# Hybrid mixer stack on one Trainium2 core: the mLSTM strand's last head held back until SSD's last masks, in the order of steps that the engines share

## The reference, cut to what matters

```python
x = x + 0.5 * swiglu(rms_norm(x, ffn1_norm[l]), ...)
u = rms_norm(x, mix_norm[l]) @ w_in[l]
y = concatenate([ssd_mixer(u_ssd), mlstm_mixer(u_ml), rwkv7_mixer(u_rw)])
x = x + y @ w_out[l]
x = x + 0.5 * swiglu(rms_norm(x, ffn2_norm[l]), ...)
```

```python
h = num / jnp.maximum(jnp.abs(den), jnp.exp(-m_t))[..., None]
h = h.reshape(bsz, t, H, Dh) * o
return group_rms_norm(h.reshape(bsz, t, MLSTM_WIDTH), norm_g, H)
```

## Time and profile before

| | us |
|---|---|
| time, median of 3 runs | 1778.43 (1778.34 to 1779.82) |
| the profiled execution | 1779.76 |
| its span in the profile | 1777.8 |
| PE busy | 1712.3 (96%) |
| DVE busy | 1292.2 (73%) |
| ACT busy | 931.8 (52%) |
| POOL busy | 409.6 (23%) |

### The profile page before, as it was taken

How to read it: one execution, slowest core, us unless ns; L and a number is a source line. 1 busy time by engine, 2 the same in 40 slices (tenths; PEclk the granted TensorE clock), 3 DMA queues, 4 the chain that set the end, 5 groups by cost and what they waited for, 6 DMA issues and landing times.

```text
span 1777.8 us, 32695 instructions
## 1 busy us (share of the span) xinstructions
PE 1712.3 (96%) x13812; PEld 1538.4 (87%) x13812; DVE 1292.2 (73%) x2137; ACT 931.8 (52%) x1666; POOL 409.6 (23%) x316
## 2 busy tenths in 40 slices
PE   8999999999899999999999999989999999989998
PEld 6888988887798888888898888779888898979987
DVE  5887775856667887688777576566787666789974
ACT  5774435323446764577443532344676445556652
POOL 2772000000213761167200000021376200021110
PEclk9999999999799999999999999989999999989999
DMA  6675622211146664666562221114665543335442
GB/s 253 241 273 192 218 95 96 81 41 49 49 156 254 236 237 173 220 247 224 190 215 95 95 96 32 44 49 168 225 247 200 196 173 119 119 143 187 172 153 105
DMA packets 45057, 282.67 MB, mean 159 GB/s; under 512 B 6128, under 2 KB 6768, under 8 KB 18544
## 3 DMA queue, kind: packets, MB, share of 16 engines
q1 hardware_dynamic: 44912, 280.60, 43.8%
HBM read 279.53 MB, written 1.05 MB: 158 GB/s over the span
## 4 chain that ended last, share of the span: by engine, by line
PE 83%; DVE 11%; ACT 3%; issue 1%; DMA 1%; POOL 0%; SPq 0%; DVEq 0%; ACTq 0%
PE banks L517 27%; PE banks L518 13%; PE banks L1052 8%; PE banks L509 7%; PE banks L511 7%; PE banks L510 7%; PE banks L1659 4%; DVE WL L486 2%; ACT WH L481 2%; PE banks L1928 1%; DVE XC L1121 1%; PE banks L556 1%; DMA ring<-wst 1%; PE banks L1938 0%; PE banks L724 0%
## 5 line engine op out<-in xcount | busy, mean ns | idle before, releaser
L486 DVE TENSOR_TENSOR WL<-ring,WH 128x2048 fp32r<-128x2048 f32 (+1 forms) x223 | 469.0, 2114 | 119.4 <-ACT WH L481 119.2
L517 PE MATMUL banks<-XNP,WH 128*128 128x512 f32 x1408 | 498.6, 399 | 10.8 <-DVE XNP L602 8.6
L481 ACT ACTIVATE WH<-ring 128x2048 fp32r<-128x2048 f32 (+1 forms) x223 | 381.0, 1716 | 59.0 <-PE banks L511 46.6
L518 PE MATMUL banks<-XNP,WL 128*128 128x256 f32 x1408 | 393.9, 280 | 0.0
L517 PEld LDWEIGHTS banks<-XNP,WH 128*128 128x128 f32 x1408 | 266.7, 189 | 72.3 <-DVE XNP L602 9.1
L950 POOL TENSOR_TENSOR HP<-G,HP 128x256 fp32r<-128x256 f32 x110 | 210.2, 1912 | 307.6 <-ACT HP L762 307.6
L517 PE MATMUL banks<-HP,WH 128*128 128x512 f32 x770 | 267.5, 392 | 0.8 <-POOL HP L950 0.7
L518 PEld LDWEIGHTS banks<-XNP,WL 128*128 128x128 f32 x1408 | 267.1, 190 | 0.0
L518 PE MATMUL banks<-HP,WL 128*128 128x256 f32 x770 | 215.7, 280 | 0.0
L1052 PE MATMUL banks<-XN,ring 128*128 128x256 f32 x832 | 200.0, 389 | 0.0
L517 PEld LDWEIGHTS banks<-HP,WH 128*128 128x128 f32 x770 | 144.6, 188 | 33.1 <-POOL HP L950 1.4
(11 more groups left out here) (495 smaller groups left out, 3281.1 us busy)
## 6 DMA issues: line engine op xcount, KB each, us to landing
ring<-wst SPq DMA_DIRECT2D x205, 1024.0 KB, 4.8
ring<-wst SPq DMA_DIRECT2D x80, 704.0 KB, 4.2
LP<-lp SPq DMA_DIRECT2D x1, 1872.0 KB, 7.6
LP<-lp SPq DMA_DIRECT2D x4, 448.0 KB, 5.6
ring<-wst SPq DMA_DIRECT2D x2, 512.0 KB, 5.6
X<-xin SPq DMA_DIRECT2D x2, 512.0 KB, 6.3
out<-X SPq DMA_DIRECT2D x4, 256.0 KB, 2.2
C<-cst SPq DMA_DIRECT2D x1, 193.0 KB, 5.0
```

Source lines behind the costliest of these rows:

```text
L481: e.do.activation(WH[:, slot[q], 0:n], ring[:, i % NSLOT, 0:n], ACT.Copy).then_inc(*w_act.up("high", q))
L486: e.do.tensor_tensor(WL[:, slot[q], 0:n], ring[:, i % NSLOT, 0:n], WH[:, slot[q], 0:n].bitcast(F32), ALU.subtract).then_inc(*w_dve.up("low ...
L517: e.do.matmul(b[:, :], WH[:, s, cols], x.rearrange("p s t -> p (s t)"), start=first, stop=False)
L518: return e.do.matmul(b[:, 0:T], WL[:, s, cols], x[:, 0, :], start=False, stop=last)
```

## The change

One condition in `order_of`: step 42 of `scan` may stand in the list only when 23 steps of `ssd` stand ahead of it.

```diff
             if k == 42:
-                return done["proj"] >= tile_done(31)
+                return done["proj"] >= tile_done(31) and done["ssd"] >= 23
```

## The result

| | before | after |
|---|---|---|
| median of 20 runs each, us | 1778.57 (1776.43 to 1781.4) | 1784.1 (1781.58 to 1787.7) |
| ratio, with its 95% interval | | 1.0031 (1.0024 to 1.0038) |
| the profiled execution | 1779.76 | 1786.27 |
| its span | 1777.8 | 1784.3 |

The change costs 5.5 us by the medians, 0.31%. The forecast was 4.3 us and 1782.7; the time lies in its range and on the side to which it gave the greatest chance. The median stands for no typical execution, though: ten of the twenty took 1781.58 to 1783.2 and ten 1785.0 to 1787.7, so it lies in the gap between two groups whose own medians are 3.4 and 7.7 us above that of before. The profiled execution is one of the longer group.

A forecast was written before the change was run, and what follows sets the result against it. PE held 83% of the chain and DVE 11%, with PE waiting for DVE in places. First stretch 1.4 plus tail 2.9 gave 4.3 us slower, 1778.43 + 4.3 = 1782.7 us; range 1777.0 to 1786.5.

The forecast's parts named there:

- The stall that goes: Mixers: without scan.42 ahead of ssd.21's L2047, PE's L1928 starts 3.2 us earlier; 3.3 us gained by 445.85.
- The new wait: Mixers: scan.43 on ACT waits for scan.42 ahead of lane 3's copy, so PE waits 2.4 us for that copy.
- The clock in the first stretch: Up to the weight copy, both layers: 3.05 us gained at high clock to 2.85 lost at low; 1.4 lost taken.
- The tail: End of the mixers, up to L2063: 2.05 us slower per layer at the low clock; 2.9 taken for both.
- L1415 gone ahead of the gate: End of the mixers: scan.48 leaves its place ahead of SSD's gate, 0.8 us off.
- gate and squares: SSD's gate L2054: 0.5 us off with POOL free, of which SSD's squares on POOL give back 0.15.
- the root: SSD's root starts 3.65 us later because DVE waits in scan.48; 3.2 lost, as PE came 0.43 late before.
- nobody waits for its two POOL subtractions before ahead.1: Tail: POOL's two subtractions come behind SSD's squares and nobody waits for them before ahead.1; no cost given.
- Behind L2063: End of each mixer stage: nothing is moved there, so the tail's sum goes through to the end; no term of its own.
- The tail's wait is covered: Rival: the lanes set the stage's end, so the insertion of 3.2 costs nothing; -0.9 us, 1777.5; chance 0.10.
- The clock stays high in the first stretch: Rival: high clock there, tail as priced; +1.05 us, 1779.5, within 0.2%; chance 0.28 with mixtures.
- Faster: Rival: PE's clock stays high in both stretches; -3.95 us, 1774.5; chance 0.08.

The follow-up runs named there:

- experiment 3: Changed kernel with scan.43 (ACT's squares) moved back behind lane 3's step 15, right ahead of proj.81: 1777.77 us, ratio 0.9997 against the kernel before.
- experiment 6: Changed kernel plus five unread matmuls behind projection tile 39, where PE waits for lane 3's copy: 1779.8 us, ratio 1.0005 against the kernel before.
- after again: The changed kernel executed once more with nothing edited: 1782.39 us, span 1780.4.
- Experiment 12: Changed kernel with POOL's last low part of mLSTM (L1447, tile 10) waiting until SSD's root is done: one execution, 1782.08 us.
- experiment 1: Kernel before with scan.46 held back until ahead has begun, giving only the end of the mixers the changed order: 1780.52 us, ratio 1.0012.
- experiment 2: Changed kernel with scan.48 moved from ahead of SSD's root (ssd.28) to behind it: 1779.43 us, ratio 1.0006 against the kernel before.
- Experiment 11: Changed kernel plus unread matmuls in both stretches, five behind projection tile 39 and ten ahead of lane2.19: 1778.19 us, ratio 0.9998 against the kernel before.
- experiment 4: Changed kernel plus ten unread 128x256 matmuls in PE's idle stretch ahead of lane2.19: 1781.43 us, ratio 1.002 against the kernel before.
- experiment 8: Changed kernel with scan.43 ahead of proj.81, scan.48 behind ssd.28 and ten unread matmuls ahead of lane2.19: 1770.39 us, ratio 0.9946 against the kernel before.
- experiment 5: Kernel before plus twelve unread 128x256 matmuls in PE's idle stretch ahead of lane2.19: 1778.22 us, ratio 0.9995.

## Why the prediction was right, step by step

**The stall that goes.** As forecast. L1928 expected 2.24 us behind the first L1786 (440.45 - 438.21), measured 2.25; scan.42 expected at 7.64, measured 7.64.

**The new wait.** As forecast in place, cause and size: 2.4 expected, 2.34 measured; experiment 3 takes the wait away by one move. At the high clock the copy was to come at 19.69; with the clock kept high until the sums were through (experiment 6) it came at 20.17 / 19.71.

**The clock in the first stretch.** The term was 1.4 us lost over both layers, between 3.05 gained and 2.85 lost. Measured: 0.87 + 2.62 = 3.5 lost in the profiled execution, a little outside the low end, and 1.27 gained with 0.58 lost, 0.7 gained, in the other. So the bounds were right to 0.65 us, and the value between them isn't one number: it depends on the execution. What lies beyond the bound comes from the lane steps ahead of the sums, which I had priced at the high clock; the clock fell before them, and the sums start at 15.22 instead of 14.28.

**The tail.** 2.05 us a layer forecast at the low clock, 2.52 measured (20.22 against 17.70 from the copy to L2063); after again, with the last L556 nearly at the high clock, 1.6 and 1.8, where I had 1.15. Term by term: L1415 gone ahead of the gate, 0.78 (forecast 0.8); gate and squares 0.53 (forecast 0.35); the root 3.85 later behind L1950's start (forecast 3.65). From these 3.65 I took off the 0.43 us that PE was late before. It didn't come back: root to L2063 takes 4.31, as before.

**What took it is the step that failed in the tail.** Of scan.49 I said that nobody waits for its two POOL subtractions before ahead.1. Nobody does, yet one of them slows the root: I had priced such an overlap for L2054 and put it at nothing here. L528, the third instruction of SSD's root, took 0.57 us instead of 0.16 in both executions of after: both of its inputs lie in the SBUF tile SM, and it ends at 478.26, when POOL's L1447 ends at 478.23. The one-input L526 just ahead of it kept its 0.17. The root's own time before, for comparison:

```profile
473.67 0.16 DVE L524 TENSOR_SCALAR SM<-banks 128x4 f32<-128x4 f32 x1 [1.07 <-PE banks L1950]
473.86 0.17 DVE L526 TENSOR_SCALAR SM<-SM 128x4 int32<-128x4 int32 x1
474.07 0.16 DVE L528 TENSOR_TENSOR SM<-SM 128x4 f32<-128x4 f32 x1
```

The Trainium skill, page "SBUF — State Buffer" (section "Who interferes with whom"), has this as a rule: "A DVE instruction with two SBUF inputs contends with a GpSimd instruction that reads SBUF". The trace agrees, with 0.41 us for one such instruction. Experiment 12 shows the cause: with that POOL instruction behind the root, L528 takes 0.16.

**Behind L2063** I said that nothing is moved and the sum goes through. Nothing is moved, but the low clock went on: until 485.3, where before it had ended at 478.4, so the lanes' last steps ran at it and L1815 came 1.06 and 1.25 us later still (0.83 and 0.92 in after again). This is the largest term that was missing, 2.3 us in the profiled execution and 1.75 in the other against 0.8 for L528. I had ended the accounts of the low clock at the last moved instruction instead of at the point where the clock comes back.

**The sum.** Measured, first stretch, tail and what is behind L2063 add up to 3.5 + 5.0 + 2.3 = 10.8 us in the profiled execution and to -0.7 + 3.4 + 1.75 = 4.45 in the other; the median of 5.5 lies between, nearer to the second. It also lies between the two groups of the result (3.4 and 7.7), in a gap where no execution does. The forecast of 4.3 took mixed values for the first two and had nothing for the third, so its nearness to 5.5 is partly luck. My comparison with the profiled before hid a second uncertainty: in the third block that execution was 3.4 us longer than another one of the same kernel (205.9 against 202.5).

**The rivals.** "The tail's wait is covered" fell with experiments 1 and 2: the order of the tail alone costs 2.1 us, its undoing gives 4.4. "The clock stays high in the first stretch" is half right: it is a matter of the execution, and where it was made to hold (experiment 6) the change cost 0.05% (-0.04 to 0.14), the "within 0.2%" of that case, which I had at 1.05 us or 0.06%. Unread matmuls held it there, not the order of steps itself. "Faster" asked for the high clock in both stretches. Experiment 11 came nearest to it and gave 0.9998 instead of the 0.9978 of that case; it isn't a full test, as the clock was low at the first layer's last L556 even there.

## What to carry to other kernels

When a step is held back in a shared order, look at what the strand's later steps now stand in front of: here a square on ACT in front of a copy of 0.2 us, and a scale on DVE in front of another strand's root. Those two places cost more than the removed stall gave, and moving just these two steps turned +0.31% into -0.40%. A step that nobody waits for can still slow what runs beside it. Follow a low clock to the point where it comes back, not to the last moved instruction, and take two executions before a few microseconds of it are put down to a kernel.

## What the runs showed of the hardware that was not expected

- The same program with the same waits (2.34 us idle in both) had its sixteen one-column matmuls in 3.57 us in one execution and in 2.36 in another; over a whole mixer stage this was 3.3 us in the first layer and 3.1 in the second.
- The clock fell to 1.2 GHz (0.50) behind a stretch in which PE counts as busy without a gap: in the second layer of before it was 1.00 from 1154 to 1158, PE busy for all 4 us, the last work the one-column sums and SSD's products, and 0.50 from 1158. And where it was low PE can count as busy all through (452 to 460 in after, 8.00 of 8.00). PE's busy share doesn't tell it; the time of one load does (0.116 against 0.222 us).
- Matmuls that nobody reads kept the clock at 1.00 through windows of 10 to 15 us in the tail (experiments 4, 8 and the first layer of 5), but in experiment 6 it fell 1.8 us behind the start of the first layer's sums, and in experiment 11 it was low again at the last L556 of the first layer. They were worth anything from nothing that can be told (before) over 2.0 us (tail of after) to 4.6 (first stretch of after), each with its 2 us. In the tail PE then waited 0.94 to 1.09 us for the next releaser, POOL's L2081.
- A DVE instruction of 128x4 with two inputs took 0.57 us instead of 0.16 beside one POOL instruction of 128x256; it stands in a chain of nine small ones that PE waits for, so in after all of the 0.41 us is on the path. Moving the POOL instruction away took it off, but the overlap then fell on a DVE pair, 1.28 us instead of 0.75, and half of the gain was gone.
